# Suffix sums of stick-breaking attention in two split passes; the last norm shared with GpSimd

## The reference

```python
def stick_breaking(q, k, v):                       # layer 1, 8 heads of 64, 512 tokens
    z = einsum('bqhd,bkhd->bhqk', q_blk, k) * scale
    causal = s_pos[None, :] < t_pos[:, None]
    log_1m = where(causal, log_sigmoid(-z), 0.0)
    suffix = cumsum(log_1m, axis=3, reverse=True)  # over the keys, from the right
    excl = pad(suffix[..., 1:], ...)
    att = where(causal, exp(log_sigmoid(z) + excl), 0.0)
    return einsum('bhqk,bkhd->bqhd', att, v)

# end of every sub-layer, here the last one of the program:
yf = swiglu(hf, ffn_w1[layer], ffn_w3[layer], ffn_w2[layer])
x = layer_norm(RES_ALPHA * x + (1.0 + g_f) * yf, ln_g[layer, 1], ln_b[layer, 1])
# layer_norm: (x - mean) * rsqrt(var + eps) * g + b, over the 1024 features of a token
```

## Time and profile before

| | |
|---|---|
| median of 3 runs | 1439.79 us |
| the profiled execution | 1437.54 us, of which the span is 1435.7 us |
| granted TensorE clock, mean | 0.972 |
| PE busy | 1361.7 us (95%) |
| PEld busy | 1127.2 us (79%) |
| DVE busy | 634.7 us (44%) |
| POOL busy | 509.7 us (36%) |
| ACT busy | 458.2 us (32%) |

### The profile page before, as it was taken

The page is one execution under the profiler, slowest core; times in us unless marked ns, Lnnn a source line. Parts: engine busy times, 40 slices in busy tenths (PEclk is TensorE's granted clock), DMA queues, the critical chain, the costliest instruction groups (busy, mean ns, idle before and its releaser), DMA issues.

```text
span 1435.7 us, 17180 instructions
## 1 busy us (share of the span) xinstructions
PE 1361.7 (95%) x6566; PEld 1127.2 (79%) x6566; DVE 634.7 (44%) x820; ACT 458.2 (32%) x622; POOL 509.7 (36%) x209
## 2 busy tenths in 40 slices
PE   7899999889999999999899999998889999999995
PEld 6778878678888888888778777887788888887884
DVE  3579747578434344201882344357483101100007
ACT  2343344533232322112323244405243323222121
POOL 2343322323453444443253222110235444444440
PEclk9999999999999999999999999989999999999998
DMA  9592536422555465732245311111113223334212
GB/s 332 153 118 89 205 118 132 169 81 78 187 204 190 161 215 190 184 114 88 108 147 168 104 59 49 40 45 45 59 61 118 100 94 96 102 88 146 89 59 59
DMA packets 93521, 173.81 MB, mean 121 GB/s; under 512 B 15719, under 2 KB 61943, under 8 KB 93340
## 3 DMA queue, kind: packets, MB, share of 16 engines
q1 hardware_dynamic: 90328, 169.63, 38.5%
q10 hardware_dynamic: 3140, 3.43, 0.9%
HBM read 170.87 MB, written 4.52 MB: 122 GB/s over the span
## 4 chain that ended last, share of the span: by engine, by line
PE 67%; issue 20%; POOL 6%; DVE 5%; ACT 1%; POOLq 0%; DVEq 0%; ACTq 0%
PE ps L1057 13%; PE ps L1058 13%; PE ps L1059 13%; POOL w_lo L678 6%; PE ps L1089 6%; PE ps L1091 6%; PE ps L1090 6%; PE ps L1213 1%; PE ps L1547 1%; PE ps L1214 1%; PE ps L1215 1%; PE ps L1573 1%; PE ps L1561 1%; PE ps L1558 1%; DVE rec L2241 1%
## 5 line engine op out<-in xcount | busy, mean ns | idle before, releaser
L678 POOL TENSOR_TENSOR w_lo<-raw,w_hi 128x1024 fp32r<-128x1024 f32 x205 | 509.5, 2490 | 890.8 <-ACT w_hi L698 890.3
L1057 PE MATMUL ps<-h_lo,w_hi 128*128 128x512 f32 (+2 forms) x1064 | 402.9, 379 | 15.4 <-DVE tmp L2014 6.3
L1058 PE MATMUL ps<-h_hi,w_hi 128*128 128x512 f32 (+2 forms) x1064 | 399.1, 375 | 0.0
L1059 PE MATMUL ps<-h_hi,w_lo 128*128 128x512 f32 (+2 forms) x1064 | 398.8, 375 | 0.0
L698 ACT ACTIVATE w_hi<-raw 128x1024 fp32r<-128x1024 f32 x205 | 216.0, 1056 | 491.4 <-PE ps L1091 184.5
L1057 PEld LDWEIGHTS ps<-h_lo,w_hi 128*128 128x128 f32 (+1 forms) x1064 | 204.7, 192 | 55.1 <-DVE tmp L2014 7.6
L1059 PEld LDWEIGHTS ps<-h_hi,w_lo 128*128 128x128 f32 (+1 forms) x1064 | 204.6, 192 | 35.0
L1058 PEld LDWEIGHTS ps<-h_hi,w_hi 128*128 128x128 f32 (+1 forms) x1064 | 204.9, 193 | 33.6
L2098 DVE TENSOR_TENSOR tmp<-tmp,ps 128x512 f32<-128x512 f32 x44 | 30.1, 688 | 259.6 <-PE ps L1059 259.6
L1089 PE MATMUL ps<-w_hi,hid_lo 128*128 128x512 f32 x352 | 138.2, 393 | 1.8 <-issue 0.9
L1091 PE MATMUL ps<-w_lo,hid_hi 128*128 128x512 f32 x352 | 137.9, 392 | 0.0
(11 more groups left out here) (240 smaller groups left out, 1587.0 us busy)
## 6 DMA issues: line engine op xcount, KB each, us to landing
raw<-wstream SPq DMA_DIRECT2D x205, 512.0 KB, 4.1
ada_raw<-astream SPq DMA_DIRECT2D x80, 512.0 KB, 4.4
ada_first<-astream SPq DMA_DIRECT2D x16, 256.0 KB, 7.0
ada_first<-astream SPq DMA_DIRECT2D x8, 512.0 KB, 10.4
ln_rows<-row_scratch SPq DMA_DIRECT2D x3, 1024.0 KB, 6.7
skew_scratch<-f_scratch ACTq DMA_DIRECT2D x1, 2304.0 KB
xa<-xT SPq DMA_DIRECT2D x4, 512.0 KB, 9.3
out<-xa SPq DMA_DIRECT2D x4, 512.0 KB, 3.5
```

The source lines that it names most:

```text
L678: nc.gpsimd.tensor_tensor(w_lo[:, slot, :], raw[:, slot % RAW, :], w_hi[:, slot, :].bitcast(F32), ALU.subtract).then_inc(sem("w_lo_ready"), 1)
L1057: pe.matmul(o, w_h, x_l, start=start, stop=False)
L1058: pe.matmul(o, w_h, x_h, start=False, stop=False)
L1059: return pe.matmul(o, w_l, x_h, start=False, stop=stop)
```

## The change

- The softplus of a head is split into `sp_hi` (fp32r) and `sp_lo = sp - sp_hi`; the triangle and the full matrix, whose entries are 0 and -1, are copied once into an fp32r tensor `tri_ones`. `sb_tri` now runs each of its 10 matmuls twice, with fp32r operands.
- `softplus` masks with two COPY_PREDICATED in place of the two products, then casts and subtracts. There is one `sb_sp` buffer, so from head 1 on it waits for `tri_full` of the head before.
- On ScalarE the weight splits of the interleaved pieces move from in front of the piece's evacuation to behind `sb_second(h)`, in front of `sb_first(h+1)`; after head h the slots up to two pieces ahead are split.
- In the last norm, scale and offset of token blocks 0 to 2 go to GpSimd, behind its last weight remainder. Token block 3 is finished one column half after the other on TensorE, VectorE does all of its norm in halves (`last_block`), ScalarE only its square root, and it is stored in two halves.

```diff
@@ arena
-    sb_sp = [ar(f"sb_sp{i}", [P, SC], 18176 + 2560 * i) for i in range(2)]
+    sb_sp = ar("sb_sp", [P, SC], 18176)
+    sp_lo = ar("sp_lo", [P, SC], 18176, F32R)
+    sp_hi = ar("sp_hi", [P, SC], 20736, F32R)
+    tri_ones = ar("tri_ones", [P, 2 * P], 22016, F32R)
@@ sync
-        for tb in range(TB):
+        for tb in range(TB - 1):
             sp.wait_ge(sem("out_ready"), tb + 1)
             sp.dma_start(by_chunk(out[tile_of(tb), :]), x_rows(tb)).then_inc(sem("stored"), 16)
+        for b in range(2):
+            sp.wait_ge(sem("last_ready"), b + 1)
+            sp.dma_start(by_chunk(out[tile_of(TB - 1), b * S:(b + 1) * S]), xa[:, 4 * b:4 * b + 4, TB - 1, :]).then_inc(sem("stored"), 16)
@@ gpsimd, behind the last split
+        pool.wait_ge(sem("in_rows"), 16)
+        for tb in range(TB - 1):
+            pool.wait_ge(sem("xh_ready"), TB * 3 + tb + 1)
+            nc.gpsimd.tensor_tensor(x_rows(tb), x_rows(tb), by_chunk(rows_gb[:, 0, :]), ALU.mult).then_inc(sem("scaled"), 1)
+            pool.wait_ge(sem("scaled"), tb + 1)
+            nc.gpsimd.tensor_tensor(x_rows(tb), x_rows(tb), by_chunk(rows_gb[:, 1, :]), ALU.add).then_inc(sem("out_ready"), 1)
@@ scalar, heads
         for h, part in enumerate(FILL):
-            if part == "vd0":
-                hi_until(SLOTS[part][0] + 2 + RING)
-            elif part[0] == "v":
-                ahead(part)
+            if part == "vd1":
                 v_blocks(part, v_dst[part])
-            else:
-                qk_panel(part)
+            elif part != "vd0":
+                qk_panel(part, False)
...
             sb_second(h)
+            hi_until(SLOTS[FILL[0]][0] + 2 * h + 2 + RING)
             if h + 1 < 8:
                 sb_first(h + 1)
-        hi_until(SLOTS["vd0"][0] + 4 + 2)
@@ tensor, last product
+            def last_rows(nk):
+                for b in range(2):
+                    for k in range(nk - 4, nk):
...
+                        pe.matmul(o, x_l[:, k, tile_of(3)], w_hi[:, w, part], start=k == 0, stop=False)
+                        pe.matmul(o, x_h[:, k, tile_of(3)], w_hi[:, w, part], start=False, stop=False)
+                        m = pe.matmul(o, x_h[:, k, tile_of(3)], w_lo[:, w, part], start=False, stop=k == nk - 1)
+                        if b:
+                            m.then_inc(sem("slot_done"), 1)
+                    if b == 0:
+                        m.then_inc(sem("y_half"), 1)
@@ tensor, sb_tri
+            tri, ones_ = tri_ones[:, 0:P], tri_ones[:, P:2 * P]
             for j in range(TB):
-                m = pe.matmul(pe_out, cst[:, C_TRI:C_TRI + P], sp_[:, OFS[j]:OFS[j] + WID[j]], start=False, ...)
+                for sp_ in (sp_hi, sp_lo):
+                    m = pe.matmul(psf[:, base + OFS[j]:base + OFS[j] + WID[j]], tri, sp_[:, OFS[j]:OFS[j] + WID[j]], ...)
                 for k in range(j + 1, TB):
-                    m = pe.matmul(psf[...], cst[:, C_ONES:C_ONES + P], sp_[:, OFS[k]:OFS[k] + WID[k]], ...)
+                    for sp_ in (sp_hi, sp_lo):
+                        m = pe.matmul(psf[...], ones_, sp_[:, OFS[k]:OFS[k] + WID[k]], ...)
@@ vector, last block
+            def last_block(end):
+                tb = TB - 1
+                for b in range(2):
+                    dve.wait_ge(*((sem("slot_done"), end) if b else (sem("y_half"), 1)))
+                    y = ps[:, 6 + b, :]
+                    link(V.tensor_tensor(y..., y..., gate_row(i)[:, 2 * b:2 * b + 2], ALU.mult))
+                    x = xa[:, 4 * b:4 * b + 4, tb, :]
+                    link(V.scalar_tensor_tensor(x, x, ALPHA, by_chunk(y), ALU.mult, ALU.add))
+                    ins = V.bn_stats(stats[:, 2 * tb + b, :], x)
...
+                for b in range(2):
+                    ins = V.scalar_tensor_tensor(x, x, mv[:, tb, 0:1], by_chunk(rows_gb[:, 0, b * S:(b + 1) * S]), ALU.subtract, ALU.mult)
+                dve.wait_ge(sem("std_ready"), TB * i + tb + 1)
+                link(V.reciprocal(rstd[:, tb:tb + 1], cols[:, 5, tb:tb + 1]))
+                for b in range(2):
+                    V.scalar_tensor_tensor(x, x, rstd[:, tb:tb + 1], by_chunk(rows_gb[:, 1, b * S:(b + 1) * S]), ALU.mult, ALU.add
+                                           ).then_inc(sem("last_ready"), 1)
@@ vector, softplus
-            if h >= 2:
-                dve.wait_ge(sem("tri_full"), h - 1)
+            if h >= 1:
+                dve.wait_ge(sem("tri_full"), h)
-            link(V.scalar_tensor_tensor(sp_[:], psf[:, SB_COL:SB_COL + SC], 0.0, sb_a[h % 2][:], ALU.max, ALU.add))
-            for t in diag_tiles(sp_):
-                i = V.tensor_tensor(t, t, twice(cst[:, C_KEEP:C_KEEP + P]), ALU.mult)
-            i.then_inc(sem("sp_ready"), 1)
+            link(V.scalar_tensor_tensor(sb_sp[:], psf[:, SB_COL:SB_COL + SC], 0.0, sb_a[h % 2][:], ALU.max, ALU.add))
+            for t in diag_tiles(sb_sp):
+                i = V.copy_predicated(t, twice(cst[:, C_DROP:C_DROP + P]).bitcast(U32), zero_col...)
+            link(i)
+            link(V.tensor_copy(sp_hi[:], sb_sp[:]))
+            V.tensor_tensor(sp_lo[:], sb_sp[:], sp_hi[:].bitcast(F32), ALU.subtract).then_inc(sem("sp_ready"), 1)
```

More of the change, by code:

```diff
@@ L903, in normalize @@
                 nc.scalar.activation(cols[:, 5, tb:tb + 1], mv[:, tb, 1:2], ACT.Sqrt, bias=eps_col).then_inc(sem("std_ready"), 1)
+                if i == 3 and tb == 3:
+                    return
                 act.wait_ge(sem("nmr_ready"), TB * i + tb + 1)
@@ L957, in _, with qk_panel @@
         norm(1, "down0", "qc0")
-        def qk_panel(part):
+        def qk_panel(part, splits=True):
             name, p = part[:2], int(part[2])
-            ahead(part)
+            if splits:
+                ahead(part)
             wait_full(act, part, 0)
@@ L1092, in rows_of @@
                 return m
+            def last_rows(nk):
+                for b in range(2):
+                    for k in range(nk - 4, nk):
+                        w = (first + k) % RING
+                        o, part = ps[:, 6 + b, :], slice(b * S, (b + 1) * S)
+                        pe.matmul(o, x_l[:, k, tile_of(3)], w_hi[:, w, part], start=k == 0, stop=False)
[5 more added lines that the diff above has]
+                        m.then_inc(sem("y_half"), 1)
             if opening:
@@ L1104, in out_rows @@
             for tb in range(TB):
+                if i == 3 and tb == 3:
+                    last_rows(nk)
+                    break
                 for k in range(nk - 4, nk):
@@ L1553, in sb_tri @@
             base = SB_COL
-            sp_ = sb_sp[h % 2]
             pe.wait_ge(sem("sp_ready"), h + 1)
+            tri, ones_ = tri_ones[:, 0:P], tri_ones[:, P:2 * P]
             for j in range(TB):
-                pe_out = psf[:, base + OFS[j]:base + OFS[j] + WID[j]]
-                m = pe.matmul(pe_out, cst[:, C_TRI:C_TRI + P], sp_[:, OFS[j]:OFS[j] + WID[j]], start=False,
-                              stop=j == TB - 1, skip_group_check=True)
+                for sp_ in (sp_hi, sp_lo):
+                    m = pe.matmul(psf[:, base + OFS[j]:base + OFS[j] + WID[j]], tri, sp_[:, OFS[j]:OFS[j] + WID[j]],
+                                  start=False, stop=j == TB - 1 and sp_ is sp_lo, skip_group_check=True)
                 for k in range(j + 1, TB):
-                    m = pe.matmul(psf[:, base + OFS[j] + (k - j) * P:base + OFS[j] + WID[j]], cst[:, C_ONES:C_ONES + P],
-                                  sp_[:, OFS[k]:OFS[k] + WID[k]], start=False, stop=k == TB - 1, skip_group_check=True)
+                    for sp_ in (sp_hi, sp_lo):
+                        m = pe.matmul(psf[:, base + OFS[j] + (k - j) * P:base + OFS[j] + WID[j]], ones_,
+                                      sp_[:, OFS[k]:OFS[k] + WID[k]], start=False, stop=k == TB - 1 and sp_ is sp_lo,
+                                      skip_group_check=True)
             m.then_inc(sem("tri_full"), 1)
@@ L2059, in residual @@
                                        ).then_inc(sem("nmr_ready"), 1)
+            def last_block(end):
[3 more added lines that the diff above has]
+                    y = ps[:, 6 + b, :]
+                    link(V.tensor_tensor(y.rearrange("q (a b c) -> q a b c", a=2, c=P), y.rearrange("q (a b c) -> q a b c", a=2, c=P),
+                                         gate_row(i)[:, 2 * b:2 * b + 2], ALU.mult))
+                    x = xa[:, 4 * b:4 * b + 4, tb, :]
+                    link(V.scalar_tensor_tensor(x, x, ALPHA, by_chunk(y), ALU.mult, ALU.add))
+                    ins = V.bn_stats(stats[:, 2 * tb + b, :], x)
+                link(ins)
+                V.bn_aggr(mv[:, tb, :], stats[:, 2 * tb:2 * tb + 2, :].rearrange("p a b -> p (a b)")).then_inc(sem("mv_ready"), 1)
+                dve.wait_ge(sem("mv_ready"), TB * i + tb + 1)
+                dve.wait_ge(sem("in_rows"), 16)
+                for b in range(2):
+                    x = xa[:, 4 * b:4 * b + 4, tb, :]
```

(27 more changed lines are left out.)

3 lines of the change are left out of this document (1 added, 2 removed).

## The result

The change takes 1424.74 us (median of 4 runs, 1422.96 to 1426.51) against 1439.92 before (now four runs of it): ratio 0.9896, 95% interval 0.9879 to 0.9913. The forecast was 1424.2 us. The profiled execution took 1422.96 us, its span is 1421.1.

A forecast was written before the change was run, and what follows sets the result against it. TensorE was taken to bound the heads, VectorE and the store behind it the end. Heads 12.2 + end 3.4 = 15.6 us off the median 1439.79 gave 1424.2 us, range 1418.5 to 1431.5.

The forecast's parts named there:

- TensorE is the bound of the heads: Eight heads: no row of another engine stands between TensorE's rows, so shorter TensorE work shortens the heads.
- Suffix sums 4.33 to 2.80 us, 12.2 us in all: Suffix sums on TensorE: 20 fp32r matmuls take 2.80 us a head, 1.53 less than before, 12.2 over eight heads.
- The disputed price: Suffix sums: each of eight 128-column fp32r matmuls costs its weight load, taken as 0.115 us, between bounds 0.069 and 0.22.
- Rivals 1: Suffix sums: narrow fp32r matmuls run at full streaming rate, 0.069 us; heads give 15.2, total 1421.2 us; chance 15%.
- 2 (0.22): Suffix sums: fp32r below 256 columns costs as much per column as fp32; heads give 5.5, total 1430.9 us; 15%.
- Softplus in time, cost nothing: Heads: softplus is ready 1.7 to 2.3 us before its sums start, if GpSimd is idle then; no cost.
- Rival 4: Heads: GpSimd holds cast and subtraction, softplus chain becomes the bound; 20.8 us lost, total 1445.0 us; chance 4%.
- The end, 3.4 us: Last norm and stores: VectorE ends 2.5 us earlier despite GpSimd's holds, half store saves 0.9; gain 3.4 us.
- Rival 3: Last norm: GpSimd holds nothing up, so the end gives 7.2 us, total 1420.4 us; chance 8%.

The follow-up runs named there:

- e3: The change, but with the weight splits back in front of a piece's evacuation on ScalarE: 1434.3 us, ratio 0.9970.
- e4: The change, with each of the eight 128-column suffix-sum matmuls placed in front of a wider one: 1424.0 us, ratio 0.9897.
- e6: The change, with nmr of token blocks as an operation with one tensor input and a per-partition scalar: 1413.4 us, ratio 0.9833.
- e7: e6 with token block 3 also kept in PSUM until its last operation: 1412.7 us, ratio 0.9828.
- e11: The change once more, unaltered: 1427.0 us, ratio 0.9918.

## Why the prediction was right

- **TensorE is the bound of the heads.** Right: but for ScalarE's exponential behind head 0, 1.25 us in both kernels, no other engine stands in the chain of the heads, and e3 shows what happens when one enters.
- **Suffix sums 4.33 to 2.80 us, 12.2 us in all.** Measured 2.70 and a period 1.59 shorter. The disputed price was 0.115 for a matmul of 128 columns; (2.70 - 1.88) / 8 = 0.10 on average, spacing of loads 0.11, though single starts follow each other by 0.05 and 0.11. The reason given, the weight load, is shown by the PEld rows and by the pairs in e4. Rivals 1 (0.069) and 2 (0.22) are out. The Trainium skill's 81 ns ("TensorE: Matmul & The Clock Gate", "Back-to-back issue gap") lies under the 0.10 us that a narrow fp32r matmul took here on average.
- **Softplus in time, cost nothing.** Right: 2.5 us to spare where 1.7 to 2.3 were computed; the cast took 0.83, a little under the lower of its two bounds. Rival 4's mechanism is real: in e3 it cost 9.6 us. It was the place of the splits that kept it out, as argued. What I had not seen is that the masked copies would be held as well, so that the margin ended earlier than at the cast: GpSimd had to be idle from the masks on.
- **The end, 3.4 us.** Measured 3.9. Holds of `nmr` 1.09 and 1.69 (computed 1.2 and 1.8), of the mean-and-scale row 2.93 - 1.41 = 1.5 (computed 1.8), half store 2.5 us (computed 2.6), GpSimd 2.34 to 2.40 an operation. VectorE's last operation ends 26.1 us behind the first gate product of the norm against 29.1 before, 3.0 us sooner where 2.5 were computed. Rival 3, that nothing is held, is out by these rows. With `nmr` freed (e6) the end gives another 1.6 us; with the rest freed too (e7) nothing more, since the stores bound it.
- **What was missed.** The half clock behind head 0, 3.2 us in the profiled execution. The heads' 12.7 came out as 9.6, and the total was met because the end gave 0.5 more and untouched stretches 1.1. So 1424.2 against 1424.7 is luck in part: misses cancelled in the main, and the same kernel measured again (e11) gained 11.8 us and not 15.6. That is within the stated range, but its interval, 0.9902 to 0.9935, leaves out the 0.9892 of the forecast. The trace of before showed the pause of 1.33 us, but at full clock; I did not count a lower clock there among the rivals.

## What to carry to other kernels

Before VectorE is given an operation with two SBUF inputs, look at what GpSimd does at that moment: here such an operation, even on one element per partition, waited until GpSimd's was through (0.16 us became 2.08). Move GpSimd's work in time, keep one operand in PSUM (e7), or, for small operations, pass it as a per-partition scalar (e6). The last is no general way out: of the five TENSOR_SCALAR of 128 x 1024 in the earlier trace rows, which have one tensor and such a scalar, one took 2.33 us in place of 0.75; it starts at 242.1, and GpSimd is at work from 241.8 to 244.2. When a hold is found in one place, look for the same line elsewhere: here the three unchanged norms held more than the one under study. And an fp32r matmul of 128 columns adds its weight load, 0.11 us, whatever stands next to it.

## What the runs showed of the hardware that I had not expected

- COPY_PREDICATED with mask and data in SBUF is held by GpSimd like a two-input product (4.72 us in e3 for two that take 0.79 undisturbed). TENSOR_SCALAR of 128 x 1 with a scalar from SBUF is not (0.21). The Trainium skill's "SBUF — State Buffer", "SBUF: two separate sides" says this of operations with two SBUF inputs; the runs agree and add that a per-partition scalar did not count as the second in an operation of 128 x 1.
- Behind the same pause of 1.33 us nearly equal programs ran with or without a granted clock of 1.2 GHz, worth about 3 us. The runs of one kernel differ by up to 8.3 us (e7), more than some of the effects tested here.
- Two fp32r matmuls with the same stationary matrix in a row load it twice, 0.11 us each (the PEld rows of `sp_hi` and `sp_lo`).
